# The cell scatters and one-hot quads placed ahead of the first gathered chunk, the first gates loaded by GpSimd, the dense sums begun at chunk 3 instead of 7

## The reference

```
qry = (xt @ w_query).reshape(PEER_BLOCK, PEER_HEADS, 2, PEER_KEY_DIM)
s1, s2 = scores of the two query halves against keys1, keys2
v1, i1 = lax.top_k(s1, 16);  v2, i2 = lax.top_k(s2, 16)
top_s, pos = lax.top_k(v1 + v2 over all 16 x 16 pairs, 16)
idx  = (i1 * 128 + i2) at pos
gate = softmax(top_s)
act  = gelu(einsum('td,thkd->thk', xt, expert_u[idx]))
out  = einsum('thk,thkd->td', gate * act, expert_v[idx])
```

## Time and profile before

| | |
|---|---|
| median of 3 runs | 4101.82 us |
| the profiled execution | 4101.73 us |
| its span (first to last instruction) | 4099.8 us |
| PE (TensorE matmul) busy | 3766.2 us, 92% |
| DVE (VectorE) busy | 2532.3 us, 62% |
| POOL (GpSimd) busy | 1789.6 us, 44% |
| HBM traffic | 255 GB/s over the span |

### The profile page before, as it was taken

One profiled execution on the slowest core, in us unless ns is written; L12 is line 12 of the kernel. 1 busy time (PEld: TensorE's weight loads), 2 busy tenths in 40 slices (PEclk: granted clock), 3 DMA queues, 4 the chain that ended last, 5 costly groups with the idle time before them and its releaser, 6 DMA issues. The chain is left out here.

```text
span 4099.8 us, 43527 instructions
## 1 busy us (share of the span) xinstructions
PE 3766.2 (92%) x15978; PEld 2821.7 (69%) x15978; DVE 2532.3 (62%) x5462; ACT 739.8 (18%) x1381; POOL 1789.6 (44%) x1508
## 2 busy tenths in 40 slices
PE   8999999987899999995799999999878999999947
PEld 7856788876666666652688567888766666666526
DVE  4455215838767676877844452158387677668777
ACT  2243302211000000000222433022111000000002
POOL 3001103777555455555530021037774554555665
PEclk9899999998999999997897999999989999999978
DMA  3301134549999999999623011445599999999996
GB/s 106 113 31 42 58 144 144 134 117 327 409 410 403 409 400 410 406 409 400 235 84 113 31 42 59 145 142 134 124 331 409 410 408 408 402 410 399 409 403 243
DMA packets 332164, 1047.19 MB, mean 255 GB/s; under 512 B 79024, under 2 KB 96048, under 8 KB 313008
## 3 DMA queue, kind: packets, MB, share of 16 engines
q0 software_dynamic: 184320, 537.08, 35.8%
q1 hardware_dynamic: 130576, 488.45, 31.3%
q10 hardware_dynamic: 17056, 18.88, 1.3%
HBM read 1008.49 MB, written 35.78 MB: 255 GB/s over the span
## 5 line engine op out<-in xcount | busy, mean ns | idle before, releaser
L1733 PE MATMUL bank<-v_tile,shared 128*128 128x512 f32 x2048 | 906.2, 597 | 31.9 <-DVE shared L2136 30.2
L2198 POOL DMA_INDIRECT u_rows<-in_peer_u,idx_all x512 | 673.6, 1316 | 541.1 <-DVE act_u L2093 444.5
L2105 DVE SCALAR_TENSOR_TENSOR x<-v_rows,act_w,x 128x1024 f32<-128x1024 f32 x512 | 657.8, 1285 | 349.9 <-DMA v_rows<-in_peer_v,idx_all 331.9
L2093 DVE CUSTOM_DVE_ANT_0 u_rows<-u_rows,h 128x1024 f32<-128x1024 f32 x512 | 610.0, 1221 | 194.8 <-DMA u_rows<-in_peer_u,idx_all 193.1
L1733 PEld LDWEIGHTS bank<-v_tile,shared 128*128 128x128 f32 x2048 | 391.6, 192 | 485.2 <-issue 444.6
L2198 POOL DMA_INDIRECT v_rows<-in_peer_v,idx_all x512 | 560.6, 1095 | 370.7 <-DVE x L2105 275.0
L2208 POOL DMA_INDIRECT first_cells<-first_gate,cell_all x256 | 412.6, 1612 | 593.4 <-DVEq L2085 467.0
L1721 PE MATMUL bank<-hT,bT 128*128 128x256 f32 x2048 | 452.5, 379 | 0.0
L1721 PEld LDWEIGHTS bank<-hT,bT 128*128 128x128 f32 x2048 | 388.4, 190 | 72.0 <-issue 22.0
L1625 PE MATMUL bank<-hT,ring 128*128 128x256 f32 x1536 | 341.6, 383 | 14.3 <-PEq L152 14.2
L1625 PEld LDWEIGHTS bank<-hT,ring 128*128 128x128 f32 x1536 | 293.9, 192 | 56.9 <-issue 16.2
(11 more groups left out here) (406 smaller groups left out, 4547.8 us busy)
## 6 DMA issues: line engine op xcount, KB each, us to landing
v_tile<-in_peer_v SPq DMA_DIRECT2D x256, 512.0 KB, 7.4
ring<-in_w_in_panels SPq DMA_DIRECT2D x76, 1024.0 KB
bT<-in_peer_ut SPq DMA_DIRECT2D x128, 512.0 KB, 8.1
ring<-in_peer_w_query SPq DMA_DIRECT2D x32, 1024.0 KB
aT<-in_peer_ut SPq DMA_DIRECT2D x64, 512.0 KB, 7.2
sT<-in_peer_ut SPq DMA_DIRECT2D x64, 512.0 KB, 7.0
first_cells<-zeros SPq DMA_DIRECT2D x16, 1024.0 KB, 11.0
ring<-in_w_abv SPq DMA_DIRECT2D x16, 1024.0 KB
```

The source lines that it names most:

```text
L1733: ins = mm(acc[t][part][:, :], act_pair[p % AHEAD][:, at:at + P], v_tile[:, e % DENSE, part * 512:part * 512 + 512], start=(e == 0), stop= ...
L2093: nc.vector.tensor_tensor_reduce(out=u[:, n % RINGS, :], in0=u[:, n % RINGS, :], in1=h[:, t, :], scale=1.0, scalar=0.0, op0=ALU.mult, op1= ...
L2105: stt(out=m.x[:, 2 + t, :], in0=vr[:, n % RINGS, :], scalar=act_w[:, p % 4, i:i + 1], in1=m.x[:, 2 + t, :], op0=ALU.mult, op1=ALU.add).the ...
L2198: nc.gpsimd.indirect_dma_start(out=rows[:, n % RINGS, :], out_offset=None, in_=table, in_offset=bass.IndirectOffsetOnAxis(ap=idx_all[:, t, ...
```

## The change

There are four parts.

1. In the list of steps all 32 quads stand before the first chunk. Chunks 0, 1, 2 stand among `pre(6)` to `pre(11)`, and the dense pairs are spread over chunks 3 to 58: 64/56 = 1.143 a chunk.
2. GpSimd issues all 128 scatters before its first fetch.
3. `first_gates` leaves SyncE's list. GpSimd does it after its first five fetches of `peer_u` and ahead of its first fetch of `peer_v`, with its own semaphores `gates_begun`. Its waits (four stores, 128 scatters) stay.
4. SyncE's first `v_tile` load waits for the stores that read that tile as staging (in before `first_gates` had covered that); the waits on later `gates` groups are renumbered.

```diff
-HOT_CHUNKS = 4
-GATES_AFTER = 9
 CHUNKS_BESIDE = (0, 2, 4)
-LATE_CHUNKS = 4
...
-        if head == 1 and c in (HOT_CHUNKS, HOT_CHUNKS + 1):
-            out += [("choose", PEER_HEADS + 1, 2 * (c - HOT_CHUNKS) + part) for part in range(2)]
+        if head == 1 and c in (0, 1):
+            out += [("choose", PEER_HEADS + 1, 2 * c + part) for part in range(2)]
...
     for q in range(QUADS):
         order.append(("hot", q))
-        if q % (QUADS // HOT_CHUNKS) == QUADS // HOT_CHUNKS - 1:
-            order += chunk(q // (QUADS // HOT_CHUNKS))
...
-    begun = HOT_CHUNKS
+    begun = 0
     for p in range(pairs, AHEAD):
         order.append(("pre", p))
-        if p == GATES_AFTER:
-            order.append(("first_gates",))
...
+                if p == 0:
+                    sp.wait_ge(stored[0], 16 * BLOCKS // 2)
...
+            def first_gates():
+                for k in range(2):
+                    pool.wait_ge(stored[k], 16 * BLOCKS // 2)
+                pool.wait_ge(m.scattered, 16 * TOPK * PEER_HEADS * (layer + 1))
+                for k in range(2):
+                    pool.dma_start(gates[:, k, 0:CELL_OCT], io.cells[...]...).then_inc(m.gates_begun[k], 16)
+                    pool.dma_start(gates[:, k, CELL_OCT:], dram[:, k]...).then_inc(m.gates_begun[k], 16)
...
-            late = TOPK * (PEER_HEADS - 1)
-            for n in range(late):
+            for n in range(TOPK * PEER_HEADS):
                 scatter(n)
             for n in range(RINGS):
                 fetch(n, s.u_free, u, tables[0], m.u_landed)
+            first_gates()
             for n in range(RINGS):
                 fetch(n, s.v_free, vr, tables[1], m.v_landed)
...
-                if c < LATE_CHUNKS:
-                    for n in range(TOPK // LATE_CHUNKS):
-                        scatter(late + c * TOPK // LATE_CHUNKS + n)
```

More of the change, by code:

```diff
@@ L1808, in gate_oct @@
             def gate_oct(k):
-                if k >= 2:
-                    sp.wait_ge(s.gated, 2 * OCT_PAIRS * (k - 1))
+                sp.wait_ge(s.gated, 2 * OCT_PAIRS * (k - 1))
                 sp.dma_start(gates[:, k % 2, 0:CELL_OCT], io.cells[layer, :, OCT * k:OCT * (k + 1), :].rearrange("p e t -> p (e t)")).then_inc(gate_in[k % 2], 16)
                 sp.dma_start(gates[:, k % 2, CELL_OCT:], dram[:, k].rearrange("p b e t -> p (b e t)")).then_inc(gate_in[k % 2], 16)
[L1814 to L1819, removed]
             def values(p):
@@ L1842, in _ @@
             loads = iter(range(len(sources)))
-            parts = {"gate": panel, "mix": panel, "out": panel, "query": panel, "pre": pre, "first_gates": first_gates,
+            parts = {"gate": panel, "mix": panel, "out": panel, "query": panel, "pre": pre,
                      "values": values, "load_ple": load_ple}
@@ L2128, in values @@
                     v.wait_ge(s.pre_read, p + 1)
-                    if at == 0:
-                        v.wait_ge(gate_in[o % 2], 32 * (o // 2 + 1))
+                    if at == 0 and o < 2:
+                        v.wait_ge(m.gates_begun[o], 32 * (layer + 1))
+                    elif at == 0:
+                        v.wait_ge(gate_in[o % 2], 32 * (o // 2))
                     a = act_pair[p % AHEAD].rearrange("p (e t) -> p e t", e=2)
@@ L2201, in fetch @@
                 ).then_inc(sems[n % RINGS], 16)
+            def first_gates():
[3 more added lines that the diff above has]
+                for k in range(2):
+                    pool.dma_start(gates[:, k, 0:CELL_OCT], io.cells[layer, :, OCT * k:OCT * (k + 1), :].rearrange("p e t -> p (e t)")).then_inc(m.gates_begun[k], 16)
+                    pool.dma_start(gates[:, k, CELL_OCT:], dram[:, k].rearrange("p b e t -> p (b e t)")).then_inc(m.gates_begun[k], 16)
             def scatter(n):
@@ L2241, in decoder_trunk @@
         m.scattered = ctx.enter_context(nc.semaphore("cells_scattered"))
+        m.gates_begun = [ctx.enter_context(nc.semaphore(f"gates_begun{k}")) for k in range(2)]
         m.nc, m.io, m.u_landed, m.v_landed = nc, io, swdge[:RINGS], swdge[RINGS:]
```

## The result

The changed kernel takes 4124.45 us, the median of 7 runs (4121.05 to 4134.6), against 4101.82 us beside it: ratio 1.0067, 95% interval [1.0052, 1.0081]. Measured once more later: 1.0064 [1.0049, 1.008]. The ratio goes by all runs of either kernel, and the medians alone are 22.6 us apart. By the ratio the change costs 26 to 27 us, some 13.5 in each layer, where 8 in all were forecast. That is outside the half per cent that I called no change, and inside the range from 4062 to 4148 us.

What follows compares the result with a forecast made beforehand. The prediction took the stage gathering rows beside dense pairs to be bound by bytes at 407 GB/s. Two accounts, +6 and nil, gave +4 us a layer: 4101.7 + 8 = 4110 us, main case 4095 to 4144, eight-in-ten 4062 to 4148.

Steps and rivals of the forecast that it cites:

- The bound: Stage gathering chunks beside dense pairs: bound by bytes at 407 GB/s; PE has no part in what comes last.
- The quads: Quad stretch: DVE's 16.32 us wait goes, stalls total 9 us, last store issued at 954, 40 us earlier.
- GpSimd: the sum: Around the quads' end: first fetch slips from 915.6 to 948, store wait 13 us, gates from 968, rows landed at 996.
- What it is worth: Chunk 3's 28.6 us head start against bytes still to move: +4 us a layer, +8 in all.
- the account against it: Bytes landed by 1021 us: 35.1 MB moved in either kernel, so neither gain nor loss.
- The first account: At chunk 3's start: 14.1 MB left over, 34.7 us, against a 28.6 us head start: +6 us a layer.
- The spreading: Dense pairs at 1.143 a chunk in place of 1.231: costs nothing, since the sum of bytes is the same.
- The moved gate loads: Four first gate loads issued by GpSimd: at most 4 us more a layer, inside the bounds.
- PE is the bound: Faster rival: dense sums starting 39 us earlier are worth up to 39 a layer, 4024 us; chance 0.17.
- GpSimd held by the last store: Slower rival: chunk 1's u rows wait behind first_gates, DMA far below 407; +21 a layer, 4144 us; chance 0.22.
- The clock: Slower rival: PE waits for DVE from mid-stage and its clock drops; +32 a layer, 4166 us; chance 0.06.
- The start doesn't move: Rival: last pre steps hang on chunk 2, so dense sums start as before; 4115 us; chance 0.05.

Runs made afterwards that it cites:

- half loads: Kernels before and after, each loading only half the columns of every dense value tile: 4051.53 us (ratio 0.9886) and 4020.05 us (0.9804).
- gates_by_synce: The changed kernel with part 3 undone, SyncE loading the first gates after pre(8)'s weights: 4131.18 us, ratio 1.0063.
- rows_before_last_head: The changed kernel with chunk 0's ten row fetches before the last 16 scatters and the gates behind these: 4113.18 us, ratio 1.0034.
- dense_from_7: The changed kernel with the 64 dense pairs spread over chunks 7 to 58 again, 1.231 a chunk: 4119.87 us, ratio 1.0038.
- rows_before_and_from_7: The changed kernel with chunk 0's ten fetches before the last 16 scatters and dense pairs from chunk 7 on: 4108.3 us, ratio 1.0018.
- after_again: The changed kernel unaltered, measured once more beside the same runs of before: 4128.75 us, ratio 1.0064.
- chunks_later: The kernel before with chunks 0 to 3 after quads 15, 20, 26 and 31 in place of 7, 15, 23 and 31: 4110.54 us, ratio 1.0024.

## Why the prediction was near, and which step failed

**The bound: right.** Bytes set the length of the stage. The half loads turn the sign of the change, and a dense start 48 us later costs nothing. PE's idle time did grow after mid-stage, though two of its waits there are for ScalarE's gelus (5.77 and 4.88 us), which I had not named; and the last dense sum starts at 1927, not within a few us of 1915.

**The quads: right.** Stalls of 2.55, 3.38 and 3.39 us against 2.6, 2.5 and 3.8; DVE is done at 952.2 against 951.7; the store was issued to within 0.1 us of the forecast.

**GpSimd: the sum right, by luck, its terms not.** The first fetch came at 956.8, not 948: the 16 scatters took 41 us in place of 32.6, with waits of 5.47, 1.84 and 1.84 us among them where I had one of 3. The last store landed in under 10 us, not 12.8. The four gate loads took 0.57 to 0.58 us each, not 1.6; my bound from indirect issues (1.3 with the gap) was no bound for a plain load. The rule of the Trainium skill ("SBUF — State Buffer", section "SBUF: two separate sides") that VectorE's copies can hold up a DMA issued by GpSimd was not put to the test: beside L2197 and L2198, 0.58 us each, DVE was at the dot products of L2080 and at no such copy. That GpSimd issues the loads costs nothing here, for gates_by_synce is no faster. The rows of chunk 1 landed at 990.5, not 996.

**What it is worth: this step failed.** The head start at chunk 3 was right (31.2 us against 28.6). What fell was the account against it, "By that the gain is nil and so is the loss", on whose strength I took +4 and not +6 or more. It has 35.1 MB moved by 1021, and 30.94 MB were (238 GB/s over 130 us). The missing 4.2 MB are 10.3 us a layer at 409 GB/s, the first difference in the table. I counted what the rings and tiles would have taken in by then as though it had left the stretch full, and did not check it against a rate: 35.1 MB is 270 GB/s, but a stretch in which GpSimd sends its first row 41 us later than before (956.8 against 915.6), with one short gap while DVE does the choice and all rings are full, did not reach that. The first account, whose +6 a layer I leaned on, failed by the same bytes:

```profile
890.00:1049.62 159.62, 105.13 (x562) 93.99 (x563) 129.07 (x315) 30.49 (x57) 120.92 (x88) 0.84 0.87 296
```

```profile
890.00:1018.38 128.38, 101.64 (x542) 89.48 (x543) 89.81 (x263) 28.80 (x51) 77.84 (x60) 0.91 0.73 236
```

At the same point of the list (chunk 7 before, chunk 3 after) before had moved 47.2 MB and after 30.3. The difference is 16.9 MB, about the four chunks' 16.8 without any of the 2.65 MB of `pre` weights and `v_tile` that I had the changed kernel ahead by. At 409 GB/s that is 41.3 us against a head start of 31.2, a loss of 10.1 us a layer. rows_before_last_head shows that this is the cost of the late rows: ten fetches ahead of 16 scatters return 15.3 of the 20.7 us.

**The spreading, "I cost at nothing": the second failure.** It costs 4 to 6 us a layer. The sum of bytes is the same, but not the rate at which they are asked for when DVE pauses for a choice: at 56 chunks PE stops there too, for a gelu behind that choice. dense_from_7 undoes the spreading and with it these waits, and gives 8.2 of the 12.3 us back in that stretch, and ratio 1.0038 for 1.0067. That these waits make up the whole of the loss isn't shown. Undone together the two failures give back most of their sum (rows_before_and_from_7).

**The moved gate loads: right** that they are worth nothing to speak of.

**The rivals.** PE is the bound: refuted twice. GpSimd held by the last store: its wait was 2.50 us, and gates_by_synce refutes it; its price, +21 a layer from a chunk 3 at 1036, was not reached since chunk 3 started at 1018. The clock: the granted clock is 0.98 for 0.99 in the long stretch, and it is 0.83 in the two windows shown in which PE waits, with 16 records in 10.05 us after a wait of 13.81 at the end. That goes with the dips, and I take it for no cause of them: PE waits first, for a gelu behind DVE's choice, and the slower records come after (16 in 6.23 us behind the wait of 4.88). The start doesn't move: it moved by 36 us. The Trainium skill's ceiling of 435 GB/s ("DMA: Bandwidth & Descriptors", section "Specifications") was not reached: no 20 us of either kernel in the stage are above 417, and none of the kernels of the table has more than 412 in the 40 us behind the first 130.

**What stays open.** The 7 us that rows_before_and_from_7 is above before lie at the edge of what its interval tells from nothing. Its stage is 3.7 us longer, and the rest of the layers varies by several us between profiled executions of the same kernel (from the first layer's last rows to the second's first quad: 905.3 us in after, 914.7 in after_again). chunks_later has before's stage to 0.3 us and yet a ratio of 1.0024; its profile doesn't say why. Part 3 without part 1 was not tried: gates ahead of the value rows of chunks that stand among the quads would wait for stores that wait for these chunks. How far the two costs overlap is open too, and why dense_from_7 leaves 5.8 us less unused in the first 130 us.

## What to carry to other kernels

Where a stage is bound by bytes, write its length as bytes over the full rate plus the time in which the rate was missing, and price a change by the second term alone: here two terms of 10 and 6 us a layer explain what a start 36 us earlier did not bring. A queue issues in order, so what stands ahead of the first transfer of a ring (16 small scatters) costs the ring's fill as well as its own time. And an even spread that is "the same bytes" also sets how close the matmuls come up to the engines that feed them. With room between them the weight loads go on while VectorE does something else; here, without it, one choice on VectorE held ScalarE's exponentials, these a gelu, the gelu TensorE, and TensorE the weight loads.

## What the hardware showed that I had not expected

A plain load of 512 KB costs GpSimd 0.56 to 0.61 us to issue, an indirect fetch of 128 rows 0.93 to 1.0 at its shortest and up to 2.5, and an indirect scatter of 128 numbers 1.55 and up to 3.3 us: the smallest transfer is the dearest to issue. A store of 2 MB lands in 8.0 to 9.6 us where no gathered rows but the first five sets are beside it (after), and in 12.8 to 26.4 among the gathered chunks.
